# Second block's mixers of a two-block transformer kernel: pre-added kept blocks, scores on both row groups, both heads' values together, units in halves

## The reference, cut to what matters

```python
def _stick_breaking_attention(q, k, v):
        ...
        z = jnp.einsum('bhqd,bhkd->bhqk', q_blk, kh).astype(jnp.float32) * scale
        mask = k_pos[None, :] < q_pos[:, None]
        log_keep = jnp.where(mask, jax.nn.log_sigmoid(-z), 0.0)
        between = lax.cumsum(log_keep, axis=3, reverse=True) - log_keep
        a = jnp.where(mask, jnp.exp(jax.nn.log_sigmoid(z) + between), 0.0)
        return jnp.einsum('bhqk,bhkd->bhqd', a.astype(vh.dtype), vh)
        ...
def _mixer(h, w_in, conv_w, pool_w, pool_scale, w_out):
    proj = h @ w_in
    q, k, v, gate_b, gate_c, conv_h, pool_in = jnp.split(proj, SPLIT_POINTS, axis=-1)
    ...
    attn = _stick_breaking_attention(q, k, v)
    conv = _short_conv(gate_b, gate_c, conv_h, conv_w)
    pool = _multiscale_pool(pool_in, pool_w, pool_scale)
    return jnp.concatenate([attn, conv, pool], axis=-1) @ w_out
```

## Time and profile before

| | us |
|---|---|
| median of three runs | 2704.92 (2701.69 to 2705.34) |
| profiled execution | 2703.88 |
| its span, as the profile's rows count it | 2702.1 |
| PE busy | 2604.0 (96%) |
| DVE busy | 1268.5 (47%) |
| POOL busy | 974.3 (36%) |
| ACT busy | 931.8 (34%) |
| four head pairs of layer 0 | 1069.2 to 1244.9 of the span |

### The profile page before, as it was taken

The page is one execution under the profiler, slowest core; times in us unless marked ns, Lnnn a source line. Parts: engine busy times, 40 slices in busy tenths (PEclk is TensorE's granted clock), DMA queues, the critical chain, the costliest instruction groups (busy, mean ns, idle before and its releaser), DMA issues.

```text
span 2702.1 us, 33780 instructions
## 1 busy us (share of the span) xinstructions
PE 2604.0 (96%) x11396; PEld 2040.0 (75%) x11396; DVE 1268.5 (47%) x2013; ACT 931.8 (34%) x1304; POOL 974.3 (36%) x382
## 2 busy tenths in 40 slices
PE   6899989999999999998999999999999998999997
PEld 3777657887788887766788887788887776788886
DVE  8663525264331346568631335431346568631332
ACT  3344435334322234442422233322334343422231
POOL 1232324443344442222244443344442222244442
PEclk8999999999999999999999999999999999999999
DMA  5223622322133231112123232223221112123232
GB/s 233 69 75 112 241 95 88 115 93 91 65 105 105 93 106 50 47 54 74 58 96 117 91 105 81 69 99 106 98 98 50 55 47 78 62 93 101 93 105 74
DMA packets 67131, 249.14 MB, mean 92 GB/s; under 512 B 8416, under 2 KB 10464, under 8 KB 65920
## 3 DMA queue, kind: packets, MB, share of 16 engines
q1 hardware_dynamic: 67072, 248.39, 27.0%
HBM read 244.89 MB, written 2.10 MB: 91 GB/s over the span
## 4 chain that ended last, share of the span: by engine, by line
issue 69%; POOL 16%; PE 14%; POOLq 1%; DVE 0%; ACT 0%; DVEq 0%
POOL w_lo L412 16%; PE unit_bank L447 4%; PE unit_bank L449 4%; PE unit_bank L448 4%; PE score L530 1%; POOLq L416 1%; DVE x L1659 0%; DVE unit_bank L1657 0%; POOLq L411 0%; PE mix L496 0%; PE stat_bank L504 0%; PE out_bank L496 0%; ACT arena L861 0%; PE mix L504 0%; DVE f L1640 0%
## 5 line engine op out<-in xcount | busy, mean ns | idle before, releaser
L412 POOL TENSOR_TENSOR w_lo<-raw,w_hi 128x1024 fp32r<-128x1024 f32 (+2 forms) x378 | 974.0, 2577 | 1700.7 <-ACT w_hi L844 1700.7
L447 PE MATMUL unit_bank<-u_hi,w_hi 128*128 128x512 f32 x2160 | 856.4, 396 | 16.7 <-DVE f L1750 8.3
L448 PE MATMUL unit_bank<-u_lo,w_hi 128*128 128x512 f32 x2160 | 845.0, 391 | 0.0
L449 PE MATMUL unit_bank<-u_hi,w_lo 128*128 128x512 f32 x2160 | 844.6, 391 | 0.0
L844 ACT ACTIVATE w_hi<-raw 128x1024 fp32r<-128x1024 f32 (+2 forms) x378 | 418.4, 1107 | 1136.7 <-PE unit_bank L449 1099.3
L447 PEld LDWEIGHTS unit_bank<-u_hi,w_hi 128*128 128x128 f32 x2160 | 407.3, 189 | 122.4 <-issue 31.2
L449 PEld LDWEIGHTS unit_bank<-u_hi,w_lo 128*128 128x128 f32 x2160 | 407.6, 189 | 85.9
L448 PEld LDWEIGHTS unit_bank<-u_lo,w_hi 128*128 128x128 f32 x2160 | 407.7, 189 | 85.3 <-issue 2.9
L447 PE MATMUL unit_bank<-h_hi,w_hi 128*128 128x512 f32 x992 | 390.7, 394 | 17.1 <-POOL w_lo L412 11.8
L448 PE MATMUL unit_bank<-h_lo,w_hi 128*128 128x512 f32 x992 | 387.3, 390 | 0.0
L449 PE MATMUL unit_bank<-h_hi,w_lo 128*128 128x512 f32 x992 | 387.3, 390 | 0.0
(11 more groups left out here) (295 smaller groups left out, 2121.1 us busy)
## 6 DMA issues: line engine op xcount, KB each, us to landing
raw<-in_w_gate_up SPq DMA_DIRECT2D x168, 512.0 KB, 3.4
raw<-in_w_down SPq DMA_DIRECT2D x64, 704.0 KB, 4.1
raw<-in_w_in SPq DMA_DIRECT2D x66, 512.0 KB, 3.5
raw<-in_w_up SPq DMA_DIRECT2D x32, 512.0 KB, 3.5
raw<-in_w_out SPq DMA_DIRECT2D x24, 512.0 KB, 3.5
f<-in_w_ada_rows SPq DMA_DIRECT2D x22, 512.0 KB, 4.6
raw<-in_w_down SPq DMA_DIRECT2D x16, 512.0 KB, 3.5
ada_late<-in_w_ada_rows SPq DMA_DIRECT2D x10, 512.0 KB, 4.5
```

Of the source, the lines that this page charges most:

```text
L412: e.tensor_tensor(w_lo[:, s, 0:n], raw[:, s, 0:n], as32(w_hi[:, s, 0:n]), ALU.subtract).then_inc(lo_ready, 1)
L447: e.matmul(bank[:], wh, hi(k), start=n == 0, stop=False)
L448: e.matmul(bank[:], wh, lo(k), start=False, stop=False)
L449: mm = e.matmul(bank[:], wl, hi(k), start=False, stop=last)
```

## The change

1. *Pre-added kept blocks.* DVE adds kept blocks that meet at the same query block (three sums of 128 columns in `kept_sums`), and PE multiplies the table of ones by six pieces of 128 columns, where before it took every later block at its full width.
2. *Scores on both row groups.* SP copies q_st and k_st with their halves of 64 partitions swapped (`turn_heads`, four DMAs for each pair), and z takes every second block from the copies, so that successive blocks stand on different row groups. z(0) waits for the copies (`qk_turned`). Their place in SP's queue is between weight loads.
3. *Values of both heads side by side.* The second head's weights go to `own`, and one `values()` at the end of the pair does both heads, alternating.
4. *Halved units.* `in_half` is one half of a unit; units (2j+2, 0) and (2j+3, 0) have keep_sums between their halves. Unit (2j+2, 1) moves ahead of keep_sums(1).
5. *The order on ACT and DVE.* Refills come between the logarithms and the weights; split_out, the former end of a pair, comes after the next pair's take of f; take_q and the take of k_st come ahead of where they stood; pool(0) and pool(1) go to pairs 1 and 2. Loops over the pairs are unrolled.
6. *In every norm* the refill stands ahead of the squares of the same unit.

The diff, cut to its core:

```diff
+        q_turned, k_turned = us[:, 0, :], us[:, 1, :]
+        kept_sums = ssm_tmp[:, 0:2, :].rearrange("p n k -> p (n k)")[:, 0:3 * P].rearrange("p (n t) -> p n t", t=P)
...
+            def turn_heads(l, j):
+
+                if j == 0:
+                    e.wait_ge(first_taken, 2 * (3 * l + 1) + 2)
+                else:
+                    for h in range(2):
+                        e.wait_ge(taken[h], mix2(l) + 2 * j + 2)
+                for src, out in ((q_st, q_turned), (k_st, k_turned)):
+                    for h in range(2):
+                        e.dma_start(out[HD * h:HD * h + HD, :], src[HD - HD * h:P - HD * h, :]).then_inc(qk_turned, 16)
...
-                        load_pairs(mix2(l) + 1, d["w_in2"], 2 * MIX2_IN * l + 2, MIX2_IN - 1)
+                        for n in range(1, MIX2_IN):
+                            for h in range(2):
+                                load(mix2(l) + n, h, d["w_in2"][2 * MIX2_IN * l + 2 * n + h], D)
+                                if h == 0 and n in (2, 4, 6, 8):
+                                    turn_heads(l, n // 2 - 1)
...
+                def in_half(p, s, m):
+
+                    if m == 0:
+                        e.wait_ge(lo_ready, 2 * p + s + 1)
+                        e.wait_ge(taken[s], p + 1)
+                    for k in range(4 * m, 4 * m + 4):
+                        wh, wl = w_hi[:, s, k * P:(k + 1) * P], w_lo[:, s, k * P:(k + 1) * P]
+                        e.matmul(unit_bank[s][:], wh, u_hi[:, k, :], start=k == 0, stop=False)
+                        e.matmul(unit_bank[s][:], wh, u_lo[:, k, :], start=False, stop=False)
+                        mm = e.matmul(unit_bank[s][:], wl, u_hi[:, k, :], start=False, stop=k == DC - 1)
+                    if m:
+                        mm.then_inc(unit_done, 1)
...
-                        rows = slice(HD * h, HD * h + HD)
+                            e.wait_ge(qk_turned, 64 * (J + 1))
                         for n in range(TB):
                             i = TB - 1 - n
+                            side = (h + n) % 2
+                            rows = slice(HD * side, HD * side + HD)
+                            q, k = (q_turned, k_turned) if n % 2 else (q_st, k_st)
                             e.wait_ge(sums_taken, 8 * J + TB * h + n + 1)
-                            e.matmul(z_bank[i][:, 0:T - i * P], k_st[rows, i * P:(i + 1) * P], q_st[rows, i * P:T],
+                            e.matmul(z_bank[i][:, 0:T - i * P], k[rows, i * P:(i + 1) * P], q[rows, i * P:T],
                                      start=True, stop=True).then_inc(z_done, 1)

                     def keep_sums(h):
...
+                        below = {1: ((1, kept[:, 2, 0:P]), (2, kept_sums[:, 0, :])),
+                                 0: ((1, kept[:, 1, 0:P]), (2, kept_sums[:, 1, :]), (3, kept_sums[:, 2, :])),
+                                 2: ((1, kept[:, 3, 0:P]),), 3: ()}
                         for n in range(TB):
                             i = TB - 1 - n
                             e.wait_ge(sp_ready, 8 * J + TB * h + n + 1)
                             R = z_bank[i]
                             mm = e.matmul(R[:, 0:T - i * P], tab("after"), kept[:, i, 0:T - i * P], start=True,
                                           stop=n == 0)
-                            for m in range(i + 1, TB):
-                                mm = e.matmul(R[:, (m - i) * P:T - i * P], tab("ones"), kept[:, m, 0:T - m * P],
-                                              start=False, stop=m == TB - 1)
+                            for m, total in below[i]:
+                                mm = e.matmul(R[:, m * P:(m + 1) * P], tab("ones"), total, start=False, stop=i + m == TB - 1)
                             mm.then_inc(R_done, 1)

-                    def values(h):
-                        if h == 0:
-                            e.wait_ge(v2_ready, J + 1)
-                        e.wait_ge(a_ready, 8 * J + TB * (h + 1))
-                        rows = slice(HD * h, HD * h + HD)
+                    def values():
+                        e.wait_ge(v2_ready, J + 1)
+                        e.wait_ge(a_ready, 8 * J + 2 * TB)
                         for i in range(TB):
-                            mm = e.matmul(out_bank[rows, i * P:T], v_nat[:, i, rows], a_keys[:, i, 0:T - i * P],
-                                          start=i == 0, stop=i == TB - 1)
+                            for h in range(2):
+                                rows = slice(HD * h, HD * h + HD)
+                                mm = e.matmul(out_bank[rows, i * P:T], v_nat[:, i, rows],
+                                              (a_keys, own)[h][:, i, 0:T - i * P], start=i == 0, stop=i == TB - 1)
                         mm.then_inc(pv2_done, 1)
...
                     z(0)
                     in_unit(pm + 2 * j + 1, 1)
+                    in_half(pm + 2 * j + 2, 0, 0)
                     keep_sums(0)
                     turn_v(o2_taken, J + 1, taken[0], pm + 2 * j + 3, v2_turned)
+                    in_half(pm + 2 * j + 2, 0, 1)
                     z(1)
-                    values(0)
-                    in_unit(pm + 2 * j + 2, 0)
+                    in_unit(pm + 2 * j + 2, 1)
+                    in_half(pm + 2 * j + 3, 0, 0)
                     keep_sums(1)
-                    in_unit(pm + 2 * j + 2, 1)
-                    in_unit(pm + 2 * j + 3, 0)
-                    values(1)
+                    in_half(pm + 2 * j + 3, 0, 1)
+                    values()
...
                     for s in range(2):
+                        refill(p + i + 1, s, D if r in (2, 5) or r == 0 else RING)
                         f_squares(p + i, s, part, 2 * i + s, g)
-                        refill(p + i + 1, s, D if r in (2, 5) or r == 0 else RING)
...
                         def weights(h):
-                            if h == 1:
-                                e.wait_ge(pv2_done, 2 * J + 1)
+                            if h == 0 and J:
+                                e.wait_ge(pv2_done, J)
+                            out = (a_keys, own)[h]
                             for n in range(TB):
                                 i = TB - 1 - n
                                 e.wait_ge(sums_taken, 8 * J + TB * (h + 1) + n + 1)
-                                e.activation(a_keys[:, i, 0:T - i * P], own[:, i, 0:T - i * P],
+                                e.activation(out[:, i, 0:T - i * P], own[:, i, 0:T - i * P],
                                              ACT.Exp).then_inc(a_ready, 1)
...
-                        decay(0)
+                        sizes(0)
                         logs(0)
+                        refill(pm + 2 * j + 2, 1)
                         weights(0)
-                        refill(pm + 2 * j + 2, 1)
-                        decay(1)
+                        sizes(1)
+                        refill(pm + 2 * j + 3, 0)
                         logs(1)
-                        refill(pm + 2 * j + 3, 0)
+                        refill(pm + 2 * j + 3, 1)
                         weights(1)
-                        refill(pm + 2 * j + 3, 1)
                         refill(pm + 2 * j + 4, 0)
-                        e.wait_ge(pv2_done, 2 * J + 2)
+                        e.wait_ge(pv2_done, J + 1)
...
+                    def split_out(j):
+
+                        e.wait_ge(ohi2_ready, HEAD_PAIRS * l + j + 1)
+                        e.tensor_tensor(h_lo[:, j, :], out_bank[:], as32(h_hi[:, j, :]), ALU.subtract).then_inc(o2_taken, 1)
...
+                            ready = 8 * J + TB * h
                             for n in range(TB):
                                 i = TB - 1 - n
                                 W = T - i * P
-                                e.wait_ge(softp_ready, 8 * J + TB * h + n + 1)
+                                e.wait_ge(softp_ready, ready + n + 1)
                                 e.scalar_tensor_tensor(kept[:, i, 0:W], softp[:, i, 0:W], -1.0, kept[:, i, 0:W],
                                                        ALU.mult, ALU.subtract)
                                 step(e.tensor_tensor(own[:, i, 0:W], own[:, i, 0:W], softp[:, i, 0:W], ALU.subtract))
+                                if i == 2:
+                                    e.wait_ge(sp_ready, ready + 1)
+                                    step(e.tensor_tensor(kept_sums[:, 0, :], kept[:, 2, P:2 * P], kept[:, 3, 0:P], ALU.add))
+                                if i == 1:
+                                    e.wait_ge(sp_ready, ready + 2)
+                                    e.tensor_tensor(kept_sums[:, 1, :], kept[:, 1, P:2 * P], kept[:, 2, 0:P], ALU.add)
+                                    e.tensor_tensor(kept_sums[:, 2, :], kept[:, 1, 2 * P:3 * P], kept_sums[:, 0, :], ALU.add)
                                 e.tensor_tensor(own[:, i, 0:P], own[:, i, 0:P], mask_b[:], ALU.add)
                                 e.tensor_tensor(kept[:, i, 0:P], kept[:, i, 0:P], tab("strict"),
```

(21 more changed lines are left out.)

32 lines of the change are left out of this document (17 added, 15 removed).

## The result

The changed kernel takes 2675.36 us (median of 4 runs, 2672.47 to 2677.84) against 2704.27 us before (2701.69 to 2705.34): a ratio of 0.9894, 95% interval 0.9877 to 0.9911, 28.9 us less. The forecast was 2692 us, 13 us less. The time lies in the stated range and on the forecast side, but the gain is more than twice what was forecast.

What follows compares the result with a forecast made beforehand. TensorE, busy nearly all of the span, was taken as the bound: 2703.9 - 44.3 (PE work) - 11.7 (pairs' end) - 11.8 (norms) + 45.3 (new waits) + 8.7 (clock) + 0.8 (unit starts) = 2690.9, 2692 us against the median; range 2662 to 2709.

Steps and rivals of the forecast that it cites:

- z: Scores of each head: alternating row groups overlap and save 0.85 us per head, 13.6 us in all.
- values: Both heads' products on two column halves overlap: 4.55 to 2.4 us per pair, 17.1 us off in all.
- the end of the pairs: End of each layer's pairs: TensorE's 4.15 us wait and 1.7 us clock loss go, 11.7 us off in all.
- keep_sums' work: TensorE's keep_sums: pre-added blocks stream 512 fewer columns, 0.85 us per head, 13.6 us off in all.
- Head 1: Second head's keep_sums: splits from two refills hold up keep_logs, so PE waits 2.2 us in each pair.
- Head 0: First head's keep_sums: a split holds keep_logs about 2.2 us, so PE waits 1.0 us in each pair.
- turn_v: Pairs after a layer's first: turn_v waits 2.15 us for split_out behind add_sums(0), six times, 12.9 us added.
- rival B: keep_logs: POOL's split does not hold it up; 2654 us, or 2662 with turn's clock losses; chance 0.20.
- rival D: z or values: row groups or column halves do not overlap; 2706 or 2709 us; chance 0.05.
- The clock: Behind 16 new waits over 2 us: a third, 5, lose 1.7 us each at half clock, 8.7 us added.
- Rival C: Each of 16 new waits is followed by half clock, costing 27 or 54 us: 2710 to 2737; chance 0.12.
- rival N: Norms' down phases: refill swap gives nothing because DVE's cycle sets the pace; 2703.8 us; chance 0.10.

Runs made afterwards that it cites:

- run 5: Changed kernel with all scores of a head on its own row group, as before, copies still made and waited for: 2689.9 us.
- run 6: Changed kernel with the 16 records of values issued head after head instead of in turn: 2681.6 us.
- Run 11: Run 8's kernel with pool in four even parts and its end reordered, then keep_sums as before the change, without pre-added blocks: 2646.99 us.
- run 1: Changed kernel with ScalarE's refills moved so that GpSimd's splits run beside operations that read PSUM: 2654.28 us.
- run 3: Changed kernel with run 1's refill moves, and split_out(j-1) moved early, between parts(0) and keep_logs(0): 2648.29 us.
- run 4: Kernel before the change with only the norm swap, the refill ahead of the squares: 2687.57 us.
- run 7: Changed kernel with both pools back in the last pair: 2682.54 us.
- run 8: Run 3's kernel with each pool cut in two and one part in each pair: 2642.05 us.
- run 9: Changed kernel with keep_sums as before the change, without pre-added blocks and their three adds: 2674.36 us.

## Why the prediction was wrong, step by step

**Inside the pairs: 2.2 us less was forecast (1.2 with the wait for the copies, which lies just ahead of them), 12.7 came.**
- z, values, the end of the pairs: right in mechanism, and within 1.3 us each (table above). The 1.3 us of values are two roundings: both heads took 4.60 us and not 4.55 before, and 2.30 and not 2.4 after. Runs 5 and 6 show that each is due to what the prediction named, with the addition that a third of values' gain stays when the heads are issued one after the other.
- keep_sums' work: 0.84 us per head, forecast 0.85. But the step "4.25 us when nothing holds it up" took a second head's keep_sums for both. In before the first head's took 4.57 to 5.08; the earlier trace rows holds it, 1159.19 to turn at 1163.94. Those waits, 0.48 us x 8 = 3.8 us, went as well, and the sum has no term for them. Run 11, with the old widths, has the first head's at 4.33 us where DVE is ahead. The list of waits has no row for them in that stretch, and the prediction went by the list.
- New waits. Head 1: 2.1 us against 2.2. Head 0: 1.0 against 1.0. turn_v: 2.0 against 2.15. pool: pair 2 waits 1.4 and pair 3 2.6 us, 4.0 per layer against 2.9. In all 46.2 us by the starts, against 44.3. The copies, ahead of the pairs: 1.2 us in two waits, both before a first pair, against 1.0. So rival B, that the split does not hold keep_logs up, is out, by the rows above and by run 1; rival D is out by the table's z and values and by runs 5 and 6.
- **The clock: the term that failed.** A third of 16 waits of over 2 us was to be followed by half clock, 8.7 us. There was one such stretch in the pairs of the two layers together (us, busy of PE, PEld, DVE, ACT, POOL, PEclk, DMA share, GB/s; the stretch ahead of it, then the stretch itself, and the same place in layer 0):

```profile
2190.00:2202.00 12.00, 7.16 (x34) 5.13 (x33) 10.80 (x25) 2.90 (x5) 2.57 (x1) 1.00 0.13 44
2202.10:2205.50 3.40, 3.40 (x11) 2.83 (x12) 0.69 (x1) 0.00 (x0) 0.00 (x0) 0.52 0.00 0
...
1195.00:1209.00 14.00, 9.15 (x44) 6.61 (x44) 10.07 (x21) 1.84 (x4) 2.35 (x1) 1.00 0.12 38
```

  PE was idle for nearly 5 of 12 to 14 us in both layers' pair 3, in four waits of up to 2.0 us, and the clock fell in one layer only. It cost 1.6 us. The 7.1 us that the sum has too much are the largest single part of the miss. The count of 16 was wrong as well: only turn_v's six waits were of 2.0 us in one piece. The 2.1 us of head 1 and pool's came in pieces, none over 1.5 us in the list. Nor does the length of a single wait decide alone: runs 1, 5 and 6 had two or three such stretches in the pairs, and in run 3 three waits of 0.85 to 1.04 us were followed by 6.8 us at half clock in both layers. After waits of 4.2 to 4.5 us (runs 4, 7 and 8, and before) the clock fell each time. Rival C needed 15 or 16 stretches.
- Starts of units cost 1.4 instead of 0.8 us.

Together: 7.1 + 3.8 + values 1.3 + turn_v's own 1.0, less 1.9 for waits and 0.6 for starts, make 10.7, and the difference is 12.7 - 2.2 = 10.5 us.

**Outside: 11.8 us forecast, 15.7 measured** (run 4). The mechanism stands and rival N is out; the size came from the list of waits, which leaves about 0.3 us of each wait out. Run 4's 15.7 and the mixers' 12.7 us, less 1.2 for the copies, add up to 27.2 of the 28.9 us.

**The rule on the hold-up.** The Trainium skill, GPSIMD Engine Reference, Key points, has GpSimd and VectorE collide when a VectorE instruction has two SBUF inputs. The trace agrees in keep_logs, which no row of before could show: 2.87 us for 0.68 and 2.34 for 0.28, as above, and run 1 took the collisions away without taking an operation away.

**What stays open.** Which waits are followed by half clock: in the changed kernel the same waits in the same order did it in one layer and not in the other. The runs differ by up to one stretch of 3.4 us at other places of the span, so differences of 2 us between two kernels are not explained here.

## What to carry to other kernels

- A wait's price is read from start to start, against the same piece where nothing holds it up; the idle time in the list of waits left out 0.3 us of each wait here, and missed waits of 0.3 to 0.8 us wholly.
- Before TensorE work is taken out, ask whether the engine that feeds it is ahead: pre-adding was worth 0 us behind a late VectorE (run 9) and 11.5 to 13.7 us behind one that was ahead (run 11). And what a copy on ScalarE sets off (here GpSimd's split, 2.4 us) should run beside operations that read PSUM: that move alone was 21 us.
- After each wait that is removed, look at where the next one forms: of 13.7 us gained inside the pairs in run 8, about half was given back behind them.
